# State space with filling rows: the order of three pieces of TensorE work inside each of eight blocks

## The reference, cut to what matters

```
x_t = Lbar x_{t-1} + Bbar u_t          # complex diagonal, per group of 16 channels
y_t = Re(C x_t) + D u_t
y = s5_ssm(pad(u), a_re, a_im, log_step, b_re, b_im, c_re, c_im, d_skip)
g_s = gelu(y); glu = g_s @ w_glu + b_glu
```

## Time and profile before

| | us |
|---|---|
| median of 3 runs (1674.48 to 1682.09) | 1681.15 |
| profiled execution, its time | 1680.73 |
| profiled execution, its span | 1678.9 |
| PE busy in the span | 1621.5 (97%) |
| DVE busy | 1181.6 (70%) |
| ACT busy | 718.9 (43%) |
| POOL busy | 305.3 (18%) |
| idle of PE put down to the `toeplitz` loads | 9.0 in 4 waits |

### The profile page before, as it was taken

How to read it: one execution, slowest core, us unless ns; L and a number is a source line. 1 busy time by engine, 2 the same in 40 slices (tenths; PEclk the granted TensorE clock), 3 DMA queues, 4 the chain that set the end, 5 groups by cost and what they waited for, 6 DMA issues and landing times.

```text
span 1678.9 us, 21070 instructions
## 1 busy us (share of the span) xinstructions
PE 1621.5 (97%) x8722; PEld 1322.1 (79%) x8722; DVE 1181.6 (70%) x1636; ACT 718.9 (43%) x931; POOL 305.3 (18%) x211
## 2 busy tenths in 40 slices
PE   7999998998999999999999999999999998999997
PEld 7778787876788898888887899878746877777775
DVE  6998787755534358743556467979576747999998
ACT  5334432336322353312222234333575336777774
POOL 2022000014000000060000001334101005455551
PEclk9999999999999999999999999999999999999999
DMA  7345216851222243435335432222200107999994
GB/s 298 142 156 176 72 60 195 203 176 67 99 101 101 95 157 126 177 124 225 126 126 201 174 109 75 87 89 100 101 26 3 73 8 319 384 389 382 370 381 180
DMA packets 70542, 270.76 MB, mean 161 GB/s; under 512 B 23968, under 2 KB 32800, under 8 KB 43952
## 3 DMA queue, kind: packets, MB, share of 16 engines
q1 hardware_dynamic: 45280, 163.31, 27.6%
q0 software_dynamic: 15696, 101.87, 15.3%
q10 hardware_dynamic: 9472, 4.26, 1.0%
HBM read 244.00 MB, written 25.41 MB: 160 GB/s over the span
## 4 chain that ended last, share of the span: by engine, by line
PE 82%; DVE 8%; ACT 4%; DMA 3%; SPq 2%; issue 1%; POOL 1%; DVEq 0%; ACTq 0%; POOLq 0%
PE bank L394 80%; DVE wsplit L2867 2%; SPq L3165 2%; DMA ring<-in_wmoe,indices 1%; DVE wsplit L1867 1%; DMA toeplitz<-kpad 1%; DVE parts L2867 1%; ACT wsplit L1147 1%; ACT parts L1804 1%; ACT g_high L1406 1%; DVE block_out L2909 1%; PE bank L930 0%; DMA cst<-in_cst 0%; PE bank L1073 0%; PE bank L598 0%
## 5 line engine op out<-in xcount | busy, mean ns | idle before, releaser
L394 PE MATMUL bank<-h_high,wsplit 128*128 128x512 f32 (+1 forms) x992 | 293.3, 377 | 2.4 <-DVE wsplit L1867 1.2
L1867 DVE TENSOR_TENSOR wsplit<-ring,wsplit 128x2048 fp32r<-128x2048 f32 x82 | 190.2, 2320 | 145.7 <-ACT wsplit L1147 145.7
L1147 ACT ACTIVATE wsplit<-ring 128x2048 fp32r<-128x2048 f32 x93 | 177.7, 1910 | 181.4 <-PE bank L394 174.0
L394 PE MATMUL bank<-xn_high,wsplit 128*128 128x512 f32 (+1 forms) x832 | 221.3, 353 | 5.7 <-DVE wsplit L1867 5.6
L394 PEld LDWEIGHTS bank<-h_high,wsplit 128*128 128x128 f32 x992 | 181.2, 188 | 39.3 <-DVE wsplit L1867 2.0
L394 PE MATMUL bank<-h_low,wsplit 128*128 128x512 f32 (+1 forms) x496 | 185.0, 373 | 0.0
L394 PE MATMUL bank<-f_high,wsplit 128*128 128x512 f32 (+1 forms) x576 | 172.6, 375 | 0.2 <-DVE wsplit L1867 0.2
L394 PEld LDWEIGHTS bank<-xn_high,wsplit 128*128 128x128 f32 x832 | 148.3, 193 | 28.4 <-DVE wsplit L1867 6.0
L394 PE MATMUL bank<-xn_low,wsplit 128*128 128x512 f32 (+1 forms) x416 | 146.1, 351 | 0.0
L394 PEld LDWEIGHTS bank<-f_high,wsplit 128*128 128x128 f32 x576 | 105.5, 188 | 20.2 <-DVE wsplit L1867 0.4
L3087 POOL DMA_INDIRECT ring<-in_wmoe,indices x42 | 81.1, 1932 | 151.2 <-DVE routing L2816 96.6
(11 more groups left out here) (540 smaller groups left out, 3380.0 us busy)
## 6 DMA issues: line engine op xcount, KB each, us to landing
ring<-in_W SPq DMA_DIRECT2D x122, 1024.0 KB, 4.8
weights_out<-prep SPq DMA_DIRECT2D x8, 864.0 KB, 8.3
prep<-weights_out_early POOLq DMA_DIRECT2D x8, 576.0 KB, 3.2
toeplitz<-kpad SPq DMA_DIRECT2D x128, 32.0 KB, 2.5
xslot<-zeros SPq DMA_DIRECT2D x7, 516.0 KB, 5.0
block<-xslot SPq DMA_DIRECT2D x6, 516.0 KB, 11.2
yslot<-block_out SPq DMA_DIRECT2D x6, 512.0 KB, 8.8
prep<-turns_early POOLq DMA_DIRECT2D x8, 288.0 KB, 2.4
```

The costliest lines, as they stand in the source:

```text
L394: return g.matmul(o, l, r, start=first, stop=last_, skip_group_check=True)
L1147: g.activation(split_in(n, 0), ringt[:, n % RING, :], ACT.Copy).then_inc(*a.sig(("high", n)))
L1867: g.tensor_tensor(split_in(n, 1), ringt[:, n % RING, :], hi, SUB).then_inc(*t.sig(("low", n), ("released", n)))
```

## The change

The same work in another order. On TensorE, `across(cb-1)` moves from the head of block cb to behind `turn_weights(cb+1)`. On ScalarE, `across_out(cb-1)` and `weights_turned(cb+1)` change places accordingly. Nothing is added or removed, and the lists of VectorE, GpSimd and SyncE are untouched.

```diff
@@ -652,12 +652,12 @@
             for cb in range(8):
-                if cb:
-                    across(cb - 1)
                 into(cb)
                 within(cb)
                 if cb < 7:
                     turn_weights(cb + 1)
+                if cb:
+                    across(cb - 1)
                 one_row(*FILL[cb])
             across(7)
@@ -1388,10 +1388,10 @@
             for cb in range(8):
                 if cb < 7:
                     moduli(cb + 1)
+                if cb < 7:
+                    weights_turned(cb + 1)
                 if cb:
                     across_out(cb - 1)
-                if cb < 7:
-                    weights_turned(cb + 1)
```

## The result

| | us |
|---|---|
| before, median of 4 runs | 1681.62 |
| changed, median of 4 runs (1699.79 to 1706.40) | 1703.62 |
| ratio, 95% interval | 1.0136, 1.0113 to 1.0159 |
| changed, profiled execution: time, span | 1701.14, 1699.3 |

The change costs 22 us. The forecast was 1714 with a range of 1694 to 1726: the side and the wait in SyncE's queue were right, the loss was forecast half as large again as it is (+33.4 against 22), and of the clock's behaviour a step was wrong.

A forecast was written before the change was run, and what follows sets the result against it. Bound: TensorE's 11.7 us per block and the single toeplitz buffer's load, joined at within. Six intervals +31.7, start -2.0, end +2.0 and +1.7 make +33.4 on 1680.7: 1714 us, range 1694 to 1726.

The forecast's parts named there:

- The wait that moves: SyncE's toeplitz issue, behind the prepared load's wait for across, starts 5.2 us after within's start s, instead of 2.0.
- L: Toeplitz load's time from first issue to last landing: 11 us taken for blocks 1 to 4, 10 for 5 and 6.
- The clock: TensorE's waits of 4 us halve its clock for 6.8 us each block, putting the first toeplitz issue at s + 8.5.
- the state sustains itself: At the low clock within still waits 4.4 us, about 3.5 in blocks 5 and 6, so the clock falls every block.
- The sum: Six intervals between within(1) and within(7) take 111.7 us against 80.0, +31.7; with the ends +33.4.
- The ends: Stage's ends: within(1) starts 2.0 us earlier; across(6) behind within(7) adds 2.0, the longer low clock there 1.7.
- Nothing absorbed later: After the stage, TensorE and ScalarE work hangs on its end, so the whole delay passes on.
- Nobody waits for the earlier sums: into and scan come 2 us earlier, but states isn't read before the next block, so nobody waits for them.
- its first rival: Clock stays up, only the load waits: six intervals of 15.5 us, 1694 us; chance 0.22 including clock falls in some blocks.
- the sum's own case: Clock falls after the wait in every block, giving 1714 us; chance 0.66.
- The load that stays hidden: Toeplitz set lands within TensorE's 11.7 us of work: 1669 us, or 1681 with the old waits kept; chance 0.04.
- The banks and the late prepared load: Late prepared load delays scan's first products, TensorE waits a second time, 3 us in five blocks: 1729 us; chance 0.08.

The follow-up runs named there:

- after_store_late: Changed kernel with the DRAM store of each late u row (u 4 to 7) issued one block later, behind across_out: 1710.29 us, ratio 1.0174.
- the two toeplitz-first kernels: SyncE issues the toeplitz set ahead of the prepared load: in the changed kernel 1674.66 us, in the kernel before 1687.10 us.
- the late load: Kernel before, with the toeplitz set also waiting until ScalarE has copied the turned weights: 1691.47 us, ratio 1.0063.
- after_split: Changed kernel with the toeplitz set issued by two queues, 8 DMAs by GpSimd and 8 by SyncE still behind the prepared load: 1682.88 us, ratio 1.0014.
- after_pool: Changed kernel with all 16 toeplitz DMAs of blocks 1 to 7 issued by GpSimd: 1688.62 us, ratio 1.0051.
- e2_act_old: Changed kernel with ScalarE's order of before, across_out ahead of weights_turned: 1702.63 us, ratio 1.0122.

## Why the prediction was right, point by point

**The wait that moves: right.** The first toeplitz issue at s + 5.2 was measured at s + 5.3, right behind the prepared load. Taking the set out of that wait brought back all of the loss (1674.7), and the same delay in the old order made a loss (1691.5).

**L: right at full clock, too long at the low one.** The sets issued at full clock with a u row took 11.2 and 11.7 us (forecast 11), those issued in a slow block 9.2 and 9.0: there the row's store came behind the last issue. In blocks 5 and 6 it was 9.3 and 9.4 (forecast 10). The row's store goes with a longer L, as argued, but where it falls depends on the clock too. The estimate of 9.3 us for every L, with a landing of 2.1 us, doesn't come out of the rows: the seven sets' issuing has a mean of 7.9 us, which gives 9.6, and a sum 6 to 7 us smaller in place of 9.

**The clock: the term that was mis-sized.** The step "the state sustains itself" failed for this kernel. The wait in a slow block is the first issue plus L less TensorE's own work, forecast as 8.5 + 11 - 15.1 = 4.4 us. The first slow block had 9.45 + 9.2 - 18.0 = 0.7 (0.77 in the timeline), the second 1.34. All three terms were off. The low stretch was 13.7 us long in place of 6.8, so TensorE's own work grew to 18.0 and 17.2 us. `within`, `turn` and `across` lay wholly in it (3.43 + 1.85 + 3.68 against 2.81 + 1.56 + 3.5), so the first issue came later. And L was 9.2 and 9.0 in place of 11. The longer stretch alone wouldn't have ended it: with the forecast L the wait would have been 9.45 + 11 - 18.0 = 2.4 us, and at waits of 1.96 to 2.77 us the clock did fall every time in `after_store_late`. What remained, 0.77 and 1.34 us, didn't bring it down. So the blocks alternated. The sum had 16.2, 19.5 (three times) and 18.5 (twice), together 111.7; measured were 16.6, 18.8, 17.1, 18.6, 14.7, 17.0, together 102.8. That is 8.9 of the 13.0 us by which the forecast of +33.4 exceeded the profiled +20.4 (the two spans).

**The ends.** From `within(0)` to `within(1)` 1.3 us were gained (13.3 against 14.6), for 2.0 forecast, as the first set was waited for. From `within(7)` to `across(7)` it took 9.6 us against 9.1, +0.5 for +3.7 forecast: after a wait of only 0.66 us the clock stayed up, where it had fallen before. Those 3.2 us are the other large part of the miss. The rest nearly cancels: 0.7 us less gained ahead of `within(1)` than forecast, against 1.2 us by which the stage began earlier in this execution, which isn't the change's, and 0.4 us behind it.

**Nothing absorbed later: right.** From the start of `across(7)` to the end of the span it is 1316.0 us before and 1315.6 after.

**"Nobody waits for the earlier sums": right for the two kernels compared, too strong as a general statement.** With the prepared load issued last, the old order does wait for the states (0.69 and 2.98 us), and the new one, one block's work later, doesn't in the loop. The change may have a use, but only once the load that it delays is out of its way.

**The rivals.** What came is none of the cases that had a sum of their own. The clock fell in some blocks, which the prediction put between its first rival (1694) and its sum (1714), at 1695 to 1704, with a chance of 0.22 together with that rival; the sum's own case, to which it gave 0.66, didn't come. The load that stays hidden was refuted by the result and by the queue. The banks and the late prepared load showed no wait in any trace of the changed order.

What stays open: the 12 us between the two toeplitz-first kernels. Their profiled executions show 4.5 us between `within(1)` and `within(7)` (79.3 against 83.8), 1.8 between `within(0)` and `within(1)`, 3.0 ahead of that, where the kernels are the same, 1.0 up to `across(7)`, and 6.1 from there to the end, where `across(7)` ran at the low clock; which part is states and which is landings wasn't taken apart. Why some last landings take 3 to 6 us without a store ahead of them, and why a low stretch lasts 7 us in one place and 14 in another, isn't settled either.

## What to carry to other kernels

Before an instruction is moved on one engine, look for every queue that waits for it, and for what stands behind that wait: here the cost of a reordering on TensorE lay in a SyncE list that the change didn't touch, and swapping two calls there turned +1.4% into -0.4%. A single-buffered load whose time from release to landing equals the work that covers it has no slack, and what is lost there can come back with more on top through the clock (the late load: 14.5 us in the stage for 10 us of delay). What paid most was to halve the issue time by using a second, idle queue (-0.9%); in the changed order it brought the +1.4% down to +0.1% while one half still stood behind the wait, and to -0.8% with both halves free of it. When a loop has two speeds, work out the next pass for both, with the terms as they are at that speed, before calling one of them stable.

## What the runs showed of the hardware that wasn't expected

- Idle matmuls can pay: with 28 us of them the changed kernel was 5 to 7 us faster, with the granted clock at 1.00 over the stage.
- The clock fell after waits as short as 1.45 and 0.91 us (in `after_split`) in this loop, where short groups of small matmuls surround the wait, while the wait of 1.25 us in the kernel before, and one of 1.72 us in `after_pool` (ahead of `within(2)`), left it up. A low stretch lasted 3.4, 6.8, 10.2 or 13.7 us, and once 17.1 (`e2_act_old`, from 340.0).
- A store of 264 KB issued within 1.4 us ahead of a 32 KB load went with a landing of 3.4 to 5.5 us in place of 1.9 (six of six in the table), but landings of 4.0 and 4.2 us came without one, so it isn't the only thing that delays them.
- The part of the kernel ahead of this stage is the same in all of these kernels, but for the queue of the first `toeplitz` set in the split ones, and `into(0)` still started anywhere from 252.1 to 256.5 us in the profiled executions, so a few us of difference between two profiles are not the edit's.
